# Two transformer blocks on one core: the order of the three split products within a weight unit

## The reference, cut to what matters

```python
proj = h @ w_in[l]
y = jnp.concatenate([o_hg, o_gdn], axis=-1) @ w_out[l]
y = jnp.square(jax.nn.relu(h @ w_ff1[l])) @ w_ff2[l]
# second block: h @ w_in, mixed @ w_out, mem_n @ w_kv, h @ w_q, o @ w_o, h @ w_up, (...) @ w_down
```

## Time and profile before

| What | Value |
|---|---|
| Median of three runs | 2914.16 us (2913.7 to 2915.37) |
| The profiled execution's own time | 2917.34 us |
| Its span, first to last instruction | 2915.5 us |
| TensorE's mean granted clock in it | 0.974 of full speed |
| Matmuls and weight loads | 12554 each |
| of these from the three product lines | 3256 each of L406, L407, L408 |
| HBM read | 556.28 MB |

### The profile page before, as it was taken

One profiled execution on the slowest core, in us unless ns is written; L12 is line 12 of the kernel. 1 busy time (PEld: TensorE's weight loads), 2 busy tenths in 40 slices (PEclk: granted clock), 3 DMA queues, 4 the chain that ended last, 5 costly groups with the idle time before them and its releaser, 6 DMA issues.

```text
span 2915.5 us, 32539 instructions
## 1 busy us (share of the span) xinstructions
PE 2697.1 (93%) x12554; PEld 2186.7 (75%) x12554; DVE 1818.5 (62%) x2198; ACT 1224.7 (42%) x1560; POOL 63.7 (2%) x86
## 2 busy tenths in 40 slices
PE   4899998689799999999979999998989999999987
PEld 2378887687678888888857777777778888888876
DVE  7678677876775555555664456676455564646455
ACT  2134545333444444444444444444544434444433
POOL 1000000001000000000001000000000000000000
PEclk9899999999999999999989999999999999999998
DMA  9968885155585555555735533545345556565452
GB/s 377 336 206 274 289 305 199 35 197 205 196 287 184 186 195 188 179 189 186 253 134 182 177 126 135 170 140 174 137 161 185 191 173 199 168 199 179 161 159 99
DMA packets 154719, 562.29 MB, mean 193 GB/s; under 512 B 9688, under 2 KB 13943, under 8 KB 150768
## 3 DMA queue, kind: packets, MB, share of 16 engines
q1 hardware_dynamic: 150480, 542.15, 54.8%
q0 software_dynamic: 3952, 18.22, 1.8%
q10 hardware_dynamic: 176, 0.40, 0.1%
HBM read 556.28 MB, written 4.46 MB: 192 GB/s over the span
## 4 chain that ended last, share of the span: by engine, by line
PE 53%; issue 29%; DVE 12%; ACT 3%; DMA 3%; POOL 0%; DVEq 0%; SPq 0%; POOLq 0%; ACTq 0%
PE banks L406 15%; PE banks L407 15%; PE banks L408 15%; DMA raw_weights<-in_w_ada 3%; DVE weights_low L364 2%; ACT weights_high L351 2%; PE banks L474 1%; DVE mod_in L797 1%; PE banks L712 1%; DVE modulation L382 1%; DVE proj L1135 1%; DVE proj L1001 1%; DVE proj L985 1%; PE banks L1257 0%; PE banks L1265 0%
## 5 line engine op out<-in xcount | busy, mean ns | idle before, releaser
L364 DVE TENSOR_TENSOR weights_low<-raw_weights,weights_high 128x1024 fp32r<-128x1024 f32 (+2 forms) x846 | 989.1, 1178 | 900.6 <-ACT weights_high L351 880.1
L351 ACT ACTIVATE weights_high<-raw_weights 128x1024 fp32r<-128x1024 f32 (+2 forms) x846 | 858.0, 1021 | 1022.0 <-PE banks L408 970.7
L406 PE MATMUL banks<-weights_high,lhs_high 128*128 128x512 f32 (+1 forms) x2208 | 882.0, 399 | 28.2 <-DVE weights_low L364 20.2
L408 PE MATMUL banks<-weights_high,lhs_low 128*128 128x512 f32 (+1 forms) x2208 | 863.9, 391 | 0.0
L407 PE MATMUL banks<-weights_low,lhs_high 128*128 128x512 f32 (+1 forms) x2208 | 863.3, 391 | 0.0
L406 PEld LDWEIGHTS banks<-weights_high,lhs_high 128*128 128x128 f32 x2208 | 419.0, 190 | 122.3 <-DVE weights_low L364 21.9
L408 PEld LDWEIGHTS banks<-weights_high,lhs_low 128*128 128x128 f32 x2208 | 418.2, 189 | 86.5
L407 PEld LDWEIGHTS banks<-weights_low,lhs_high 128*128 128x128 f32 x2208 | 419.5, 190 | 80.7 <-issue 1.0
L406 PE MATMUL banks<-weights_high,hid_high 128*128 128x512 f32 x856 | 337.9, 395 | 15.9 <-DVE hid_low L2561 6.4
L408 PE MATMUL banks<-weights_high,hid_low 128*128 128x512 f32 x856 | 335.8, 392 | 0.0
L407 PE MATMUL banks<-weights_low,hid_high 128*128 128x512 f32 x856 | 335.8, 392 | 0.0
(11 more groups left out here) (409 smaller groups left out, 2043.7 us busy)
## 6 DMA issues: line engine op xcount, KB each, us to landing
raw_weights<-in_w_ff SPq DMA_DIRECT2D x128, 1024.0 KB, 5.0
raw_weights<-in_w_ada SPq DMA_DIRECT2D x96, 1024.0 KB, 6.9
raw_weights<-in_w_in SPq DMA_DIRECT2D x96, 1024.0 KB, 5.4
raw_weights<-in_w_up SPq DMA_DIRECT2D x80, 1024.0 KB, 4.9
raw_weights<-in_w_down SPq DMA_DIRECT2D x42, 1024.0 KB, 5.1
raw_weights<-in_w_out SPq DMA_DIRECT2D x32, 1024.0 KB, 5.2
first_weights<-in_w_in SPq DMA_DIRECT2D x16, 768.0 KB, 12.7
raw_weights<-in_w_ckv SPq DMA_DIRECT2D x8, 1024.0 KB, 4.9
```

What stands on the lines that cost most here:

```text
L351: act.activation(WHI[:, u % SPN, 0:c.width], RAW[:, n % RAWN, k % 2, 0:c.width], ACT.Copy).then_inc(S("high_made"), 1)
L364: dve.tensor_tensor(WLO[:, u % SPN, 0:c.width], RAW[:, n % RAWN, k % 2, 0:c.width], WHI[:, u % SPN, 0:c.width].bitcast(F32), ALU.subtract) ...
L406: nc.tensor.matmul(o, x, hi, start=(k == 0), stop=False)
L408: mm = nc.tensor.matmul(o, y, hi, start=False, stop=(k == c.kn - 1))
```

## The change

Within each half of 512 columns the six matmuls of a unit are put in another order. Before, the order was bank 2h: high·high, high·low, low·high, then bank 2h + 1: the same three. Now the product is the outer loop and the row tile the inner one: high·high to bank 2h, high·high to bank 2h + 1, high·low to both, low·high to both. The number of matmuls, their operands and shapes are the same, and so are all waits and signals, but the wait for `bank_free` of bank 2h + 1 now stands ahead of the second matmul of the half (it was ahead of the fourth), and `bank_done` of bank 2h comes with the fifth matmul (it was the third). The three lines L406, L407, L408 become one line. Nothing else in the program differs.

```diff
-                for h, w in halves:
-                    hi, lo = WHI[:, s, 512 * h:512 * h + w], WLO[:, s, 512 * h:512 * h + w]
-                    for t in range(TT):
-                        b = 2 * h + t
-                        if k == 0 and c.at["done"][b] > 0:
-                            pe.wait_ge(S(f"bank_free{b}"), val(c.at["done"][b], c.ddone[b], i))
-                        if c.tiles is None:
-                            x, y = (z[:, k, 128 * t:128 * t + 128] for z in (lh, ll))
-                        else:
-                            t0 = c.tiles[k] + 128 * t
-                            x, y = lh[:, 0, t0:t0 + 128], ll[:, 1, t0:t0 + 128]
-                        o = PS[:, b, 0:w]
-                        nc.tensor.matmul(o, x, hi, start=(k == 0), stop=False)
-                        nc.tensor.matmul(o, x, lo, start=False, stop=False)
-                        mm = nc.tensor.matmul(o, y, hi, start=False, stop=(k == c.kn - 1))
-                        if b == c.banks - 1:
-                            mm.then_inc(S("unit_used"), 1)
-                        elif k == c.kn - 1:
-                            mm.then_inc(S(f"bank_done{b}"), 1)
+                order = [(x, h, t) for h, _ in halves for x in range(3) for t in range(TT)]
+                for n, (x, h, t) in enumerate(order):
+                    b, w = 2 * h + t, halves[h][1]
+                    if k == 0 and x == 0 and c.at["done"][b] > 0:
+                        pe.wait_ge(S(f"bank_free{b}"), val(c.at["done"][b], c.ddone[b], i))
+                    left = (lh, lh, ll)[x]
+                    if c.tiles is None:
+                        left = left[:, k, 128 * t:128 * t + 128]
+                    else:
+                        t0 = c.tiles[k] + 128 * t
+                        left = left[:, x // 2, t0:t0 + 128]
+                    mm = nc.tensor.matmul(PS[:, b, 0:w], left, (WHI, WLO, WHI)[x][:, s, 512 * h:512 * h + w],
+                                          start=(k == 0 and x == 0), stop=(k == c.kn - 1 and x == 2))
+                    if n == len(order) - 1:
+                        mm.then_inc(S("unit_used"), 1)
+                    elif k == c.kn - 1 and x == 2:
+                        mm.then_inc(S(f"bank_done{b}"), 1)
```

## The result

The changed kernel is slower: 2926.51 us as the median of six runs (2924.98 to 2929.93), beside 2914.76 us for the kernel before, also in six runs. The ratio is 1.0041, with a 95% interval of 1.0031 to 1.0051: 11.8 us or 0.4% more, 9 to 15 us by the interval. The forecast was 2925 us. In a later comparison of the same pair the ratio was 1.0033 (1.0021 to 1.0045). The profiled execution took 2929.93 us, the longest of the six.

A forecast was written before the change was run, and what follows sets the result against it. TensorE, busy 93% of the span, was taken to bound the kernel. Bank waits of 6.7 + 3.0 + 1.3 + 0 = 11.0 us on 2914.2 us gave 2925 us, range 2920 to 2930.

The forecast's parts named there:

- The sum: Over the whole kernel: waits for banks at chunk starts add 6.7 + 3.0 + 1.3 + 0 = 11.0 us.
- 18 x 0.37 = 6.7 us: At 18 feed-forward loop boundaries, the second matmul waits for bank 1, making the third 0.37 us late: 6.7 us.
- 0.15 us after bank 0 was free ... 8 x 0.37 = 3.0 us: At eight boundaries outside the loops, the second matmul waits for bank 1; the third is 0.37 us late: 3.0 us.
- The third term, 5 x 0.25 = 1.3 us: At five full-clock boundaries where ScalarE empties the banks, the third matmul comes 0.25 us late: 1.3 us.
- Nothing absorbs these 11.0 us: After the chunk-start waits: TensorE's own progress sets what it waits for, so all 11.0 us stay in the total.
- Banks 0 and 2 done two matmuls later ... I count 0: Where banks are emptied: done 0.45 us later, hidden by cover; counted 0, with 1 us kept in the range.
- Unsettled stretches at 0, with -14 and +16 as ends: About 200 slower units, after stops or transposes and in the second output projection: 0 us, open from -14 to +16.
- The signs: Changed profile: 2.72 us steady unit, clock near 0.974, second-matmul idle at 31 boundaries, third about 0.9 us after first in loops.
- The 10.7 ns for every matmul: Rival, every product matmul: changing bank saves 10.7 ns each, 104 us in all, giving 2821 us; chance 0.13.
- The new stationary operand: Rival: a different stationary operand each matmul slows unsettled units by 16 us (2941), or all 846 by 68 (2993); chance 0.10.
- The clock: Rival, product stream: alternating banks drops the granted clock to 0.86, for a total of about 3286 us; chance 0.03.

## Why the prediction was right, point by point

**The sum.** Forecast 11.0 us, measured 11.8 us in the first comparison and 9.3, 8.5 and 8.5 us in the three later ones with the same waits. The account of boundaries says 8.8, and 9.2 with the 0.4 us named below. So the mechanism and the place were right, and the forecast was probably 2 us high; that the first comparison came within 1 us of it is partly luck.

**"18 x 0.37 = 6.7 us".** Measured 6.28 us, 0.35 each. The two halves of the term, the wait until bank 1 is free and the late start behind a wait, are both in the rows.

**"0.15 us after bank 0 was free ... 8 x 0.37 = 3.0 us".** This one was too large: 2.33 us, 0.29 each. I let the second matmul start 0.15 us after its bank was free, because the first does. It starts at 716.00 + 1.00 - 0.5 = 716.50, and bank 1 was free at 715.17 + 1.28 = 716.45: 0.05 us, as in the loops. What holds the first matmul of these boundaries for another 0.1 us is not the emptying; it stays open. The third term, 5 x 0.25 = 1.3 us, measured 1.10, 0.18 to 0.26 each.

**"Nothing absorbs these 11.0 us".** Wrong at three boundaries of the second net. At 2415 us in the kernel before, TensorE's idle time was put down to `weights_low` of VectorE, and I read it as TensorE's own rhythm. There ScalarE's and VectorE's work for the hidden rows sets the time, not `unit_used`, so a TensorE that comes late finds less idle time. What comes back is not the loss at these three boundaries themselves but that of the loop boundary one chunk earlier: those three had cost 0.32, 0.34 and 0.36 us, and 0.31, 0.36 and 0.38 us less idle time follow. With the old order and the moved wait it is the same (0.34, 0.32 and 0.33 lost, 0.31, 0.32 and 0.32 back). So 1.0 us of the 6.7 us term was absorbed.

**"Banks 0 and 2 done two matmuls later ... I count 0".** Nearly right, and within the 1 us kept in the range: it costs 0.5 us at three chunk starts. At the first boundary, near 187 us, ScalarE starts to empty as soon as bank 0 is done and TensorE waits for it. Before:

```profile
187.00 1.06 ACT L441 ACTIVATE proj<-banks 128x512 f32<-128x512 f32 x2
...
187.72 0.47 PE L406 MATMUL banks<-weights_high,lhs_high 128*128 128x512 f32 x1 [0.42 <-ACT proj L441]
```

and with the new order everywhere but in the first unit:

```profile
186.76 1.09 ACT L440 ACTIVATE proj<-banks 128x512 f32<-128x512 f32 x2
...
187.50 0.47 PE L407 MATMUL banks<-weights_high,lhs_high 128*128 128x512 f32 x1 [0.55 <-ACT proj L440]
```

The distance from the unit ahead is 0.81 us before and 0.94 here. It grows by the same 0.13 us in both profiles of the changed kernel, and by 0.26 and 0.14 us ahead of the chunks at 2066 and 2107 us; in the two kernels that keep the old order at a chunk's end these three stay as before to 0.01 us. At the boundary of the earlier trace rows the cover was enough. In the timeline of the changed kernel one sees how far it is used up, beside the earlier trace rows:

```profile
1147.62 1.09 ACT L438 ACTIVATE hid_rows<-banks 128x512 f32<-128x512 f32 x2 [0.27 <-PE banks L405]
1147.65 0.61 PE L405 MATMUL banks<-weights_high,hid_high 128*128 128x512 f32 x2
```

ScalarE now idles 0.27 us for bank 2 and ends both at 1148.71; they are wanted at 1149.01 and 1149.24. With VectorE's emptying moved ahead the same delay cost more, as shown above.

**Unsettled stretches at 0, with -14 and +16 as ends.** Right: 200 such units against 201, and the 160 of them that don't start a chunk are 0.24 us shorter in sum. The three unequal steps of the earlier trace rows have evened out in the changed kernel's output projection:

```profile
1931.52 0.62 PE L405 MATMUL banks<-weights_low,proj_turned 128*128 128x512 f32 x2
1931.98 1.09 PE L405 MATMUL banks<-weights_high,proj_turned 128*128 128x512 f32 x4
1932.91 0.39 PE L405 MATMUL banks<-weights_low,proj_turned 128*128 128x512 f32 x1
```

Six matmuls take 1932.91 - 1931.52 = 1.39 us, 232 ns each instead of 233. Over 28 comparable units of this stage the gain is 12 ns a unit, 0.3 us. I had named a move of these steps from 233 ns as a sign of being wrong; they did move, by 1 ns, and no term of the sum depends on it.

**The signs.** The steady step, the clock and the third matmul at 0.93 us came as written. The idle time at the second matmul with VectorE's or ScalarE's line as releaser, which I had also written down, doesn't show in the merged rows, for the reason given at the boundary; there the wait is read from the starts.

**The rivals.** The 10.7 ns for every matmul are out: the settled pace is 226.7 ns with two banks in turn and with four. What makes these matmuls 13.3 ns longer than their columns stays open; it isn't the bank. The Trainium skill, "TensorE: Matmul & The Clock Gate", section "Back-to-back issue gap", gives the 215.8 ns as the gap of an isolated matmul, which the prediction didn't say, and about 131 ns for a sustained stream of 512 columns. None of the eight kernels measured here shows either in this stream; the measured 226.7 ns stands. The new stationary operand is out by the same rows. The clock is out: 1.00 in the long stretch, and 0.972 and 0.975 as means of two profiled executions of the changed kernel, 0.974 before. The same page of the Trainium skill, section "A second HAM failure mode: psum-queue depth-cycling", tells of a bf16 kernel that cycles through banks, in which TensorE idles for short moments and the clock goes back and forth. The windows row above shows no such thing: banks in turn, a clock of 1.00, and TensorE busy for 616.66 of 620 us.

## What to carry to other kernels

When matmuls are reordered, look first at what moves with them: a wait for a bank stands ahead of a matmul and holds everything behind it, and moving it two matmuls ahead cost here as much as moving the matmuls. Where one engine hands over banks one after another, the consumer should want them in the same stagger, and better still the banks should be emptied earlier: one unit earlier gave 14.5 us, more than any order of the matmuls tried here. Measure such a loss in starts, not in busy time.

## What the runs showed of the hardware that I had not expected

A matmul behind a wait holds back the next one as well: after each of the two waits the following start came 0.33 to 0.34 us later instead of 0.227. So by these rows a second wait costs 0.1 us on top of its own length. The weight loads (PEld) of the kernel before at the boundary of the earlier trace rows show where the 0.1 us is:

```profile
1165.79 0.19 PEld L406 LDWEIGHTS banks<-weights_high,hid_high 128*128 128x128 f32 x1 [0.71 <-DVE y_rows L459]
1165.90 0.19 PEld L407 LDWEIGHTS banks<-weights_low,hid_high 128*128 128x128 f32 x1
```

The first matmul's own load starts only after the wait, at the matmul's start, and the next matmul's load follows 0.11 us later. In the settled stream the next load starts within 0.01 us of the running matmul (1200.65 and 1200.66 us). The matmul after the wait is late by just these 0.11 us.

TensorE's busy time rose at the 31 boundaries by 7.7 us with the same matmuls, since the modelled end of a matmul that stands before a wait runs on into the wait.
